# Hybrid attention and mixture-of-experts block, one core: idle products, residual stores and one weight load moved in the routing stage

## The reference, cut to what matters

```
logits = hf @ w_router + b_router;  top_vals, top_idx = top_k(logits, 4);  gates = softmax(top_vals)
for each block of up to 128 (token, expert) pairs of one expert e:
    gu = xs @ w_gate_up[e] + b_gate_up[e]
    act = (clip(up) + 1) * (gate * sigmoid(1.702 * gate))
    y  = act @ w_down[e] + b_down[e]
out = x + sum over a token's four pairs of gate * y
```

## Time and profile before

| | |
|---|---|
| median of 3 runs | 1658.39 us (1657.74 to 1658.93) |
| the profiled execution, own time | 1659.49 us |
| its span, first to last instruction | 1656.6 us |
| PE busy | 1622.7 us, 98% of the span |
| DVE busy | 1349.5 us, 81% |
| ACT busy | 1096.6 us, 66% |
| POOL busy | 302.4 us, 18% |
| mean granted clock of PE | 0.992 of full |

### The profile page before, as it was taken

One profiled execution on the slowest core, in us unless ns is written; L12 is line 12 of the kernel. 1 busy time (PEld: TensorE's weight loads), 2 busy tenths in 40 slices (PEclk: granted clock), 3 DMA queues, 4 the chain that ended last, 5 costly groups with the idle time before them and its releaser, 6 DMA issues.

```text
span 1656.6 us, 24749 instructions
## 1 busy us (share of the span) xinstructions
PE 1622.7 (98%) x8080; PEld 1341.8 (81%) x8080; DVE 1349.5 (81%) x1098; ACT 1096.6 (66%) x1002; POOL 302.4 (18%) x204
## 2 busy tenths in 40 slices
PE   8999999999988999999999999999999999999996
PEld 6797777888887788888888888888888888888885
DVE  6974555423658999999999999999999999999995
ACT  5433444322355787877887877887778878778874
POOL 0000000401006623412311112211112211112110
PEclk9999999999998999999999999999999999999999
DMA  8331222432449899999999999999999999999994
GB/s 246 111 102 51 77 77 77 131 102 87 156 175 355 321 363 393 380 389 373 367 382 387 384 383 375 364 383 386 392 378 371 366 384 385 386 377 372 376 385 126
DMA packets 115017, 483.41 MB, mean 292 GB/s; under 512 B 13371, under 2 KB 56599, under 8 KB 65687
## 3 DMA queue, kind: packets, MB, share of 16 engines
q1 hardware_dynamic: 103892, 454.43, 70.4%
q0 software_dynamic: 11088, 28.48, 8.1%
HBM read 469.51 MB, written 22.26 MB: 297 GB/s over the span
## 4 chain that ended last, share of the span: by engine, by line
PE 94%; DVE 3%; ACT 1%; issue 1%; DMA 0%; POOLq 0%; SPq 0%; ACTq 0%; DVEq 0%
PE ps L624 29%; PE ps L626 29%; PE ps L625 29%; PE ps L852 2%; PE ps L846 2%; DVE work L1405 2%; PE ps L733 1%; PE ps L753 1%; PE ps L742 1%; PE ps L882 1%; PE ps L888 0%; DMA r<-in_x 0%; PE ps L857 0%; DVE r L1413 0%; ACT zT L979 0%
## 5 line engine op out<-in xcount | busy, mean ns | idle before, releaser
L1281 DVE TENSOR_TENSOR zT<-raw,zT 128x2048 fp32r<-128x2048 f32 x96 | 217.9, 2296 | 49.4 <-ACT zT L979 49.4
L1281 DVE TENSOR_TENSOR zT<-more_raw,zT 128x2048 fp32r<-128x2048 f32 x96 | 219.9, 2291 | 13.1 <-ACT zT L979 12.9
L1281 DVE TENSOR_TENSOR w_lo<-raw,w_hi 128x2048 fp32r<-128x2048 f32 x96 | 219.3, 2288 | 4.3 <-ACT w_hi L979 1.2
L979 ACT ACTIVATE w_hi<-raw 128x2048 fp32r<-128x2048 f32 x96 | 184.2, 1919 | 53.0 <-PE ps L626 53.0
L1281 DVE TENSOR_TENSOR w_lo<-more_raw,w_hi 128x2048 fp32r<-128x2048 f32 x96 | 217.7, 2294 | 1.3 <-ACT w_hi L979 0.4
L624 PE MATMUL ps<-zT,xT 128*128 128x512 f32 x512 | 202.8, 396 | 1.1 <-DVE zT L1281 1.1
L979 ACT ACTIVATE zT<-more_raw 128x2048 fp32r<-128x2048 f32 x96 | 183.5, 1911 | 26.9 <-PE ps L626 26.9
L624 PE MATMUL ps<-w_hi,xT 128*128 128x512 f32 x512 | 199.6, 390 | 1.5 <-DVE xT L1537 1.0
L626 PE MATMUL ps<-zT,xT 128*128 128x512 f32 x512 | 199.6, 390 | 0.0
L625 PE MATMUL ps<-zT,xT 128*128 128x512 f32 x512 | 199.5, 390 | 0.0
L626 PE MATMUL ps<-w_hi,xT 128*128 128x512 f32 x512 | 199.3, 389 | 0.0
(11 more groups left out here) (265 smaller groups left out, 3285.0 us busy)
## 6 DMA issues: line engine op xcount, KB each, us to landing
more_raw<-in_w_gate_up SPq DMA_DIRECT2D x129, 1024.0 KB, 8.1
raw<-in_w_gate_up SPq DMA_DIRECT2D x127, 1024.0 KB, 8.7
raw<-in_w_down SPq DMA_DIRECT2D x65, 1024.0 KB, 8.5
more_raw<-in_w_down SPq DMA_DIRECT2D x63, 1024.0 KB, 7.9
raw<-in_w_in SPq DMA_DIRECT2D x29, 1024.0 KB, 5.4
r<-in_x SPq DMA_DIRECT2D x8, 512.0 KB, 6.3
raw<-in_w_branch_conv SPq DMA_DIRECT2D x4, 1024.0 KB, 4.9
raw<-in_w_out SPq DMA_DIRECT2D x4, 1024.0 KB, 5.0
```

The source lines that it names most:

```text
L979: nc.scalar.activation(expert_pair(0, c), chunk, ACT.Copy).then_inc(split_hi, 2)
L1281: nc.vector.tensor_tensor(expert_pair(1, c), chunk, expert_pair(0, c).bitcast(F32), ALU.subtract).then_inc(split_lo, 2)
```

## The change

Four edits, in one stage.

- The 14 idle products in one place become 33 in four: 16 behind the turning of the logits, 3 behind the ranks, 4 behind the first `early_rows`, and 10 where the 14 were.
- SP loads the seventh chunk of expert 0 (chunk 6) ahead of the four h2 stores and no longer behind them.
- DVE splits chunk 2 behind the low halves of the gathered rows and no longer ahead of them.
- POOL waits for the first gather to land before it issues the five residual stores, and so before all that stands behind them in its queue.

```diff
-BUSY = 14
+BUSY = (16, 3, 4, 10)
@@ SP
             up_bias(0)
+            load_expert(0, XRAW, 0)
             for b in range(NB):
                 sp.wait_ge(h2_d if b < 2 else h2_a, b % 2 + 1)
                 sp.dma_start(h2_v[:, b, :], h2[:, b, :]).then_inc(h2_out, 16)
-            for c in range(XRAW, 8):
+            for c in range(XRAW + 1, 8):
                 load_expert(0, c, 0)
@@ PE
+            def keep_busy(n):
+
+                for _ in range(n):
+                    pe.matmul(ps[:, bk_D, :], oT[:, 0, 0, 0:P], oT[:, 0, 1, :], start=True, stop=True)
+
             pe.wait_ge(logitsT_ok, 1)
             pe.transpose(ps[:, 1, 0:P], lgT, ident).then_inc(logit_rows_pe, 1)
+            keep_busy(BUSY[0])
...
             last.then_inc(ranks_pe, 1)
+            keep_busy(BUSY[1])
...
             early_rows(0).then_inc(turned_pe, 1)
+            keep_busy(BUSY[2])
             pe.wait_ge(turned_read, 1)
...
             pe.wait_ge(early_ok, 1)
-            for _ in range(BUSY):
-                pe.matmul(ps[:, bk_D, :], oT[:, 0, 0, 0:P], oT[:, 0, 1, :], start=True, stop=True)
+            keep_busy(BUSY[3])
             pe.wait_ge(xs_in, 16)
@@ DVE
-            split_expert(0, 2)
             for half in range(2):
                 ve.wait_ge(turned_hi, half + 1)
...
+            split_expert(0, 2)
             split_expert(0, 3)
@@ POOL
             gather()
+            gp.wait_ge(xs_in, 16)
             gp.wait_ge(freed["dve"], FREED[EV[("wo", 4 * NB - 1)]][1])
             for b in range(NB):
                 gp.dma_start(out_v[:, b, :], x2[:, b, :]).then_inc(out_set, 16)
```

## The result

The changed kernel takes 1660.72 us in the median of 20 runs, against 1658.38 for the kernel before beside it: ratio 1.0016, 95% interval 1.001 to 1.0022, so 2.3 us more. That is near the 1661.1 forecast and within the 0.2% bound. What the median hides is the spread: the kernel before lies between 1656.6 and 1659.4, the changed one between 1657.7 and 1664.8.

A forecast was written before the change was run, and what follows sets the result against it. It took PE's routing stage, held by the idle products, and then POOL's slot table at block 2 as the bounds. 1659.49 + 0.3 (table) + 2.4 (clock) = 1662.2 profiled, 1661.1 us for the median; range 1655.0 to 1664.5.

The forecast's parts named there:

- the idle products held the stage: Routing: the 14 idle products, 6.09 us, hold the stage by 3.1 us, as the gather had landed at 506.2.
- 4.0 forecast, bounds 3.0 to 4.4: Routing: PE turns the gathered rows 4.0 us earlier, near 505.3 instead of 509.28, and block 0 starts at 507.3.
- 5.3 us stop at block 2: Block 2: PE's stop for the slot table grows from 1.05 to about 5.3 us, spending the 4 us gained.
- Cost: nothing: POOL's queue: waiting for the first gather costs nothing, as block 1's rows land by 519.2, before PE wants them at 523.15.
- a wait near 523: Block 1: a sign against the forecast, PE waiting for block 1's rows, which would break that cover.
- 3.9 us: Routing: estimated landing time of the first gather without the residual stores against it, with 4.8 us as a ceiling.
- the table's term: POOL's chain up to block 2: the slot table comes 0.3 us later, bounds -3.5 to +2.5.
- the wait of 0.90 us: POOL's wait for PE before the fourth scatter: said to go, with the next scatters then meeting DVE's block 1.
- the items that no longer slip through: POOL's 15 operations: only about four, not six, escape DVE's splits; two or three more at up to 2.2 us each.
- The price of 2.4 us: Block 2: cost of the clock falling to half in PE's longer stop, 2.4 us, floor 0, ceiling 2.9 to 3.5.
- Rival 4: Routing: the clock is not held, ten products run at half, block 0 starts 2 us earlier only; 1658 to 1661, 5%.
- rival 3: Block 2: the table is late by +1.5 or more and the clock falls; 1663 to 1664.5 us, 20%.

The follow-up runs named there:

- e0: The changed kernel again, no edit, one execution for a second profile: 1661.37 us.
- e2: The changed kernel without POOL's wait for the first gather: 1662.56 us, ratio 1.0028 to the kernel before.
- f1: The kernel before with only DVE's move, chunk 2 split behind the low halves: 1664.49 us, ratio 1.004.
- e1: The changed kernel with the gather of block 1's rows issued ahead of the five residual stores: 1658.87 us, ratio 1.0003 to the kernel before.
- e3: The kernel before with only the idle products spread (16, 3, 4, 10): 1657.55 us, ratio 1.0001.
- f2: The kernel before with only POOL's wait for the first gather: 1658.68 us, ratio 1.0007.
- f3: The changed kernel without POOL's wait and without DVE's move: 1655.71 us, ratio 0.9988 to the kernel before.
- f4: e3 with ACT splitting a block's third weight chunk ahead of store_y from block 2 on: 1656.68 us, ratio 0.9999 to the kernel before.
- g3: The kernel before with only DVE's block offsets moved ahead of the split of chunk 2: 1657.42 us, ratio 0.9994.
- g4: f3 with ACT splitting a block's third chunk ahead of store_y: 1656.39 us, ratio 0.999 to the kernel before.

## Why the prediction was right or wrong

**Right.** That the idle products held the stage, and that 10 in place of 14 at a fuller clock let block 0 start earlier: 2.8 and 3.6 us in the two profiles, 4.0 forecast, bounds 3.0 to 4.4. The full clock through the routing, on which this rested, held in e0 and not in the first profile. That the gather would be released by its index. That the gain does not get through, but turns into a stop of PE long enough to endanger the clock, so that the kernel ends slower by a few us: +2.3 for +2.7. The 5.3 us stop at block 2 is not in the changed kernel (0.71 and 0.51 us). It is the next wait in line: e2 and f1 show it, with the clock lost (6.3 and 6.35 us).

**Wrong: the step "Cost: nothing" of POOL's wait.** It took "even a landing of 10 us" as the cover for block 1's rows, though it named a wait near 523 as what would break it. In the changed kernel it took 18.37 us, and in e0 19.1 or a little less (508.98 to 528.11). PE stopped 3.00 and 4.44 us, 50 us ahead of where I looked. The row that bore on it was in reach: the first gather's 4.8 us was no scale for a gather behind five stores of 512 KB, and the kernel before's own landing, 10.8 us, was for stores that had left 3 us earlier. e1, where that gather goes first, and e2, where the stores go early, both have no such stop, so the late rows come from the wait and from the stores ahead in the queue. Nor did the wait buy the "3.9 us" landing of the first gather, with 4.8 as a ceiling: that landed in 4.89 us with the wait and in 5.3 without it (e2).

**Wrong: the table's term, "+0.3 us, bounds -3.5 to +2.5".** I counted place_records and the scatters as one chain from DVE's offsets. It has a second start: the gather of block 2's rows, which waits for PE. As long as POOL is there first, the table comes 36.0 to 37.4 us behind that gather (before, after, e0, e1, e3, f2, f3, f4, g3, g4), and so follows PE; only if place_records and three scatters are later than PE does their lateness count, and then it is 39.5 to 39.8 (f1, e2). I named the wait of 0.90 us and dismissed it. So what I called the table's fixed place was a consequence, and the stop at block 2 is not "1.05 + 4.0 + 0.3" for every early PE: with DVE's old order it stays at 0.67 us (f3) and 1.22 us (e3), and in f3 the gain gets through to the median; in e3 it shows in the fastest runs only. The term's number came out (the copy at 572.06, against 572.33 before) by luck: PE's stop at block 1 had given POOL the time.

**Wrong: the step that DVE's move costs nothing but the items that no longer slip through.** I put it at two or three items against 1.7 us gained. In the changed kernel five of the 15 ended with a split, four before, so the last was done at 528.4, 0.8 us later than before, while PE was to be 3 us earlier. By itself the move costs 6.1 us (f1), with the other edits 6.9 (f3 to e2). In the changed kernel this cost is hidden, since PE stops for block 1's rows anyway and POOL catches up in that time (0.90 us ahead of PE at 535.16 again). So each of the two edits covers for the other: taking out the wait alone gains nothing (e2). The kernel without both is 5.0 us faster (f3), clear of noise; the wait without the move, beside spread products, was not tried.

**The clock.** The price of 2.4 us was about right: the slow stretch of e0 cost 2.1 us. The forecast put it at block 2; in e0 it was paid at block 1, and in the first profile at neither. The Trainium skill, TensorE: Matmul & The Clock Gate, section Why this matters for your kernels, asks for no idle gaps between bursts of matmuls, at the price of a halved clock. The traces of e0, e2 and f1 agree: behind stops of 4.44, 6.3 and 6.35 us PE worked at 0.5. The stop of 3.00 us in the first profile left the clock at full. Rival 4 came true in part in the first profile (ten products at half speed, but block 0 2.8 us earlier and not 2) and not in e0.

**The number.** That 1661.1 came so near 1660.72 is in good part luck. The same gain was spent and the same clock endangered, but at another place, block 1's rows, which the sum had at nothing; and the place where the sum put the stop stayed quiet. Two small slips have no weight in it: PE waits 0.55 us at 584.48, behind the place where it was said to wait no longer for over half a microsecond, and rival 3 with a third of the forecast is a chance of 0.32, not 0.34.

**Open.** What makes single runs of the versions with spread products 3 to 5 us longer than their fastest is not settled; two executions of the changed kernel were profiled. The granted clock of the slow ones is often lower (0.991 against 0.995), so a lost clock may have a part, but 1663.99 at 0.993 stands beside 1659.23 at 0.993.

## What to carry to other kernels

A stage that gets faster hands its gain to the next fixed point; find it by asking of every queue what it must have done by then, and in which order: here block 1's rows, then the slot table. A transfer's landing is to be read from a row with the same queue in front of it, not from the same instruction in an empty one. And work that is moved out of an engine's idle time (DVE's split of 2.28 us, which had stood where DVE waits for the rows anyway) is paid for by whoever stands behind its new place, even where the move makes the path in view shorter.

## What the runs showed of the hardware

- A scatter issued by POOL takes 0.96 us with DVE free and 1.9 us, one per split, with DVE splitting without a gap, so a delay grows by steps of a split. In e2 POOL was 3.1 us late at the gather ahead of the fourth scatter, and the copy came 5.7 us later, counted from block 0's start (39.77 us from that gather to the copy; before: 37.19).
- A gather of 128 rows landed in 4.8 us with no stores ahead in its queue (before). Behind the five stores it took 8.9, 10.8 and 11.6 us where the first of them had left 8.0, 8.1 and 5.4 us earlier (f1, before, e2), and 18.37 us where it had left 3.0 us earlier (after), while the DMA engines moved 418 to 425 GB/s in all from 512 to 528.
- Stops of PE of 3.00 us (after) left the clock at full; of 4.44 (e0) and 6.3 us (e2, f1) did not. The length of one stop does not settle it: in e1 the clock fell behind a stop of 1.83 us, in the one of 0.96 us that followed, and in the routing of the changed kernel it fell near 501.9 with no stop of over 0.3 us since 493.4 in one profile and held in the other.
